# In every step of the attention loop, VectorE makes the low parts of the step behind before the present score's row maximum

## The reference, cut to what matters

```
s_cmp = einsum('bsghd,bcgd->bsghc', qg, kcmp) * scale      # compressed keys
p_cmp = masked_softmax(s_cmp, cmp_mask)
imp = einsum('bsgc,cn->bsgn', p_cmp.sum(axis=3), overlap)  # importance of 64-token blocks
_, sel_idx = lax.top_k(imp, 8)
s_sel = einsum('bqghd,bgqkd->bqghk', q_b, k_sel) * scale   # the 8 chosen blocks
s_w   = einsum('bqghd,bkgd->bqghk', q_b, k_w) * scale      # a window of 512 tokens
o = g[0] * o_cmp + g[1] * o_sel + g[2] * o_w
```

## Time and profile before

| what | value |
|---|---|
| median of three timed runs | 3189.26 us |
| profiled execution, its own time | 3188.89 us |
| its span | 3187.2 us |
| TensorE matmul busy, share of span | 3064.1 us, 96% |
| TensorE weight load busy | 2489.2 us, 78% |
| VectorE busy | 1985.1 us, 62% |
| ScalarE busy | 1339.1 us, 42% |
| GpSimd busy | 1898.0 us, 60% |
| granted TensorE clock, mean | 0.992 |

### The profile page before, as it was taken

One profiled execution on the slowest core, in us unless ns is written; L12 is line 12 of the kernel. 1 busy time (PEld: TensorE's weight loads), 2 busy tenths in 40 slices (PEclk: granted clock), 3 DMA queues, 4 the chain that ended last, 5 costly groups with the idle time before them and its releaser, 6 DMA issues.

```text
span 3187.2 us, 40487 instructions
## 1 busy us (share of the span) xinstructions
PE 3064.1 (96%) x14709; PEld 2489.2 (78%) x14709; DVE 1985.1 (62%) x2563; ACT 1339.1 (42%) x2285; POOL 1898.0 (60%) x1601
## 2 busy tenths in 40 slices
PE   8999999998999999999999999999989999999998
PEld 6888887676787888788778788867668778878887
DVE  7872256887757565655678532678775765466555
ACT  2124414766314555433320342257661345564333
POOL 3557632324456777998745585323333578889985
PEclk8999999999999999999999999999999999999999
DMA  7454551001433666644334447200005335575432
GB/s 254 151 164 128 152 132 27 1 1 34 174 91 113 212 211 211 214 158 149 128 132 139 145 146 187 73 8 1 34 21 180 110 121 184 170 235 205 155 116 106
DMA packets 378861, 412.04 MB, mean 129 GB/s; under 512 B 13355, under 2 KB 302375, under 8 KB 374312
## 3 DMA queue, kind: packets, MB, share of 16 engines
q1 hardware_dynamic: 327922, 274.77, 28.5%
q10 hardware_dynamic: 50742, 134.68, 11.9%
HBM read 294.06 MB, written 108.00 MB: 126 GB/s over the span
## 4 chain that ended last, share of the span: by engine, by line
PE 66%; DVE 13%; POOL 9%; DMA 5%; issue 3%; ACT 3%; SPq 0%; ACTq 0%; POOLq 0%; DVEq 0%
PE lin L1603 26%; PE lin L1722 24%; POOL wsum L1512 4%; POOL unit L1516 4%; PE aux L1896 2%; DVE pTL L2895 2%; DMA xraw<-in_w_ff 2%; PE lin L2038 2%; DMA wraw<-in_w_ff 2%; DVE negm L2871 2%; PE pv L1912 2%; PE pv L1913 1%; PE lin L1872 1%; PE lin L1943 1%; DVE adared L760 1%
## 5 line engine op out<-in xcount | busy, mean ns | idle before, releaser
L1722 PE MATMUL lin<-hH,unit 128*128 128x512 f32 x1712 | 565.7, 394 | 17.2 <-ACT fbuf L2440 6.6
L1443 POOL TENSOR_SCALAR unit<-wraw 128x512 fp32r<-128x512 f32 x228 | 188.0, 825 | 563.2 <-PE lin L1603 262.3
L1722 PEld LDWEIGHTS lin<-hH,unit 128*128 128x128 f32 x1712 | 323.9, 189 | 90.1 <-issue 15.4
L1516 POOL TENSOR_TENSOR unit<-wsum,unit 128x512 fp32r<-128x512 f32 x226 | 326.1, 1443 | 62.6 <-ACT unit L2161 62.0
L1445 POOL TENSOR_TENSOR wlo<-wraw,unit 128x512 fp32r<-128x512 f32 x228 | 337.9, 1482 | 19.0
L1722 PE MATMUL lin<-hL,unit 128*128 128x512 f32 x856 | 335.4, 392 | 0.0
L3079 DVE SCALAR_TENSOR_TENSOR xT<-lin,adac,xT 128x512 f32<-128x512 f32 x256 | 186.7, 746 | 216.0 <-PE lin L1722 192.2
L1603 PE MATMUL lin<-hH,unit 128*128 128x512 f32 x928 | 301.0, 394 | 5.6 <-POOL wlo L1445 5.6
L1603 PE MATMUL lin<-hL,unit 128*128 128x512 f32 x928 | 296.8, 390 | 0.0
L1603 PE MATMUL lin<-hH,wlo 128*128 128x512 f32 x928 | 296.6, 390 | 0.0
L1461 POOL TENSOR_SCALAR prob<-prob,fac 128x640 f32<-128x640 f32 (+3 forms) x128 | 112.8, 881 | 296.8 <-DVE fac L2865 287.8
(11 more groups left out here) (432 smaller groups left out, 7548.6 us busy)
## 6 DMA issues: line engine op xcount, KB each, us to landing
wraw<-in_w_ff SPq DMA_DIRECT2D x110, 512.0 KB, 6.4
wraw<-in_w_in SPq DMA_DIRECT2D x72, 512.0 KB, 5.0
wraw<-in_w_ada SPq DMA_DIRECT2D x56, 512.0 KB, 4.4
hid_keep<-ropes ACTq DMA_DIRECT2D x28, 1024.0 KB, 8.4
hN<-hid_keep SPq DMA_DIRECT2D x24, 1024.0 KB, 7.2
mix_keep<-tmp ACTq DMA_DIRECT2D x32, 512.0 KB, 6.0
hid_keep<-fbuf ACTq DMA_DIRECT2D x14, 1024.0 KB, 4.3
xraw<-in_w_ff SPq DMA_DIRECT2D x26, 512.0 KB, 8.7
```

The lines of the kernel that those rows point to most:

```text
L1443: pool.tensor_scalar(high, raw, 1.0, 1.0, ALU.mult, ALU.mult).then_inc(w_hi, 1)
L1516: pool.tensor_tensor(wide_part(n, i, 1), x, wide_part(n, i, 0).bitcast(F32), ALU.subtract).then_inc(form_lo, 1)
L1722: mm = pe.matmul(bank, w[:, k * P:(k + 1) * P], m[:, k, :], start=WIDE_BEGINS[i] and w is wh and m is mh and k == 0, stop=w is wl and k == ...
```

## The change

In step u VectorE's program now begins with the low parts of the groups of step u-1 (they stand at L2887 in the changed kernel), and the row maximum of unit u (or the three operations of a `c` unit) comes second. Before, it was the other way round. The waits are the same, and so are all instructions; TensorE, ScalarE, GpSimd and the DMA queues have the same rows in the same order as before.

```diff
                 for u in range(len(STEPS)):
+                    for x in STEPS[u - 1] if u else []:
+                        if x["kind"] != "b":
+
+                            r = SEEN[x["qt"]] if x["kind"] == "c" else P
+                            dve.wait_ge(t_hi, past["t_hi"] + x["v_no"] + 1)
+                            dve.tensor_tensor(pt("low", x, r), turned(x, r), pt("high", x, r).bitcast(F32),
+                                              ALU.subtract).then_inc(t_free[x["bank"]], 1)
                     if 0 < u < len(UNITS):
                         if UNITS[u][0] == "c":
                             dve.wait_ge(s_done, past["s_done"] + u + 2)
...
                             maximum(u)
                     if u == 2:
                         v_low("vs", vs, pv[:, :, :].rearrange("p g n -> p (g n)")).then_inc(v_lo, 2)
-                    for x in STEPS[u - 1] if u else []:
-                        if x["kind"] != "b":
-
-                            r = SEEN[x["qt"]] if x["kind"] == "c" else P
-                            dve.wait_ge(t_hi, past["t_hi"] + x["v_no"] + 1)
-                            dve.tensor_tensor(pt("low", x, r), turned(x, r), pt("high", x, r).bitcast(F32),
-                                              ALU.subtract).then_inc(t_free[x["bank"]], 1)
                     for st in SETS:
                         if st["last"] + 1 == u:
                             factors(st)
```

## The result

The changed kernel takes 3316.7 us (median of four runs, 3314.19 to 3323.1) beside 3188.03 us for the kernel before on the same chip. The ratio over all runs is 1.0408 (that of the two medians 1.0404), with a 95% interval of 1.0394 to 1.0422: 4.1% slower, where 3301 us and the range 3260 to 3345 had been forecast. The profiled execution has a span of 3311.9 us, 124.7 more than before.

What follows compares the result with a forecast made beforehand. TensorE sets the pace with VectorE close behind, but the change closes a ring through ScalarE and VectorE. 62 + 8 - 14 = +56 us per layer, +112 for two, on 3188.9 gives 3301 us, range 3260 to 3345.

Steps and rivals of the forecast that it cites:

- The ring: Floor under steps with groups: exponential, high parts, low parts, next maximum, next exponential; 3.49 us at 640 columns, two groups.
- Term 1: The 90 attention steps with groups per layer lengthen from 224.1 us to at least 286.1: +62.0 us per layer.
- the floor of 286.1: Least time in us per layer for the 90 steps with groups: exponentials 64.8, maxima 72.6, the rest 148.8.
- Term 2: Steps where VectorE's other work exceeds ScalarE's part, mainly three with compressed probabilities per layer: +8 us, bounds 6 to 12.
- Term 3: The 44 steps without groups per layer, 23 right behind a step with groups, shrink: -14 us, bounds 0 and -20.
- The clock: Rival: TensorE's share in attention drops and its clock halves in a quarter of the stage; 3400 us, chance 0.05.
- The drain rule: VectorE's next operation waits until the one ahead leaves the pipeline: 0.08 us more per handover, 12 us per layer, 3325 us.
- The rival for faster: TensorE's 16.6 us per layer of attention waits for low parts vanish and decide: 3156 us, chance 0.03.

Runs made afterwards that it cites:

- the singles' kernel: In the changed kernel, low parts go ahead of the maximum only in steps with exactly one, behind it otherwise; 3247.6 us, ratio 1.0181 to the kernel before.

## Why the prediction was right

- **The ring.** As predicted, and to 0.03 us where nothing else intrudes: 3.46 us at 640 columns and two groups (3.49 worked out), 3.94 at 896 (3.96), 2.86 with one group at 640 (2.89). The run of fifteen steps from 21 to 36 took 55.5 us; 54.1 had been added up, and 43.1 had been the time before. The shortened maximum, the shortened low part and the single low part first each change the step by what the ring says, and giving the maximum of the next unit instead opens it. In the first layer 62 of the 90 steps with groups take between 0.08 us less than their ring and 0.02 more. (The run from step 21 to 36 is not the whole run of steps with groups, as the description of the kernel has it: step 20 has one group too. The sum over the fifteen is not touched by that.)
- **Term 1, +62.0.** The 90 steps with groups took 303.7 us in the first layer, 17.6 above the floor of 286.1. The floor itself held; the 17.6 are in the next points, less about 2 for handovers that were 0.03 us shorter than taken.
- **Term 2, +8.** Too large: the six steps behind compressed units ran 4.6 us over their floor, and a smaller one 0.5. After its maximum VectorE began the compressed probabilities at once, and they took 3.3 us to the first low part instead of 3.9. One row makes up most of that, L2823. Its time in the kernel before, then the changed kernel's time line:

```profile
610.16 1.06 DVE L2823 TENSOR_TENSOR tmp<-tmp,cst 128x376 f32<-128x376 f32 x1
```

```profile
631.06 0.53 DVE L2812 TENSOR_REDUCE cst<-tmp 128x8 f32<-128x376 f32 x1
...
631.87 0.55 DVE L2823 TENSOR_TENSOR tmp<-tmp,cst 128x376 f32<-128x376 f32 x1
...
634.03 0.43 DVE L2920 TENSOR_TENSOR atL<-tmp,atH 128x256 fp32r<-128x256 f32 x1
634.37 1.28 DVE L2887 TENSOR_TENSOR pTL<-aux,pTH 128x512 fp32r<-128x512 f32 x2
635.57 1.08 DVE L2871 TENSOR_REDUCE negm<-lin 128x1 f32<-128x896 f32 x1
```

  This step takes 5.45 us beside 5.38 before: here the new order costs 0.07 us. With L2823 as long as before it would be about 0.5 us more, an estimate from these two rows. The prediction had no term for a row that changes its own length.
- **Term 3, -14.** The term that was mis-sized. The 44 steps without groups went from 64.7 to 49.3 us, -15.4, as sized. But "the step after needs a score that waits for the exponential before, so some comes back" was nearly all: the steps with groups that follow a step without ran 10 us over their floor. Step 54 of the changed kernel (ScalarE, TensorE and ScalarE again):

```profile
710.58 0.79 ACT L2351 ACTIVATE prob<-lin,negm 128x640 f32<-128x640 f32 x1 [1.18 <-DVE negm L2871]
...
711.52 0.50 PE L1872 MATMUL lin<-ksH,qS 128*128 128x512 f32 x1 [0.37 <-ACT prob L2351]
...
711.65 0.79 ACT L2351 ACTIVATE prob<-lin,negm 128x640 f32<-128x640 f32 x1 [0.18 <-DVE negm L2871]
...
712.74 0.60 PE L1891 MATMUL aux<-ident,tmp 128*39 128x128 f32 x4
...
713.37 0.59 ACT L2382 ACTIVATE pTH<-aux 39x512 fp32r<-39x512 f32 x1 [0.84 <-PE aux L1891]
```

  Step 53 was quick, 1.07 us. But its exponential frees the bank for the next score, the transposition is queued behind that score, and the high part waits 0.84 us for it. The same wait of the high part stands in 12 of the 23 steps of this kind, 8.5 us in all, and makes up most of the 10. Net, term 3 is about -5.
- **The clock** was a rival with 0.05, and in part it came. In the changed kernel's attention it fell to 1.2 GHz for 3 to 7 us at a time, five times in the first layer (about 24 us in all) and seven in the second. The first of them:

```profile
555.00:560.00 5.00, 3.72 (x24) 3.10 (x23) 3.17 (x5) 1.91 (x5) 0.00 (x0) 0.86 0.00 0
560.00:565.00 5.00, 5.00 (x17) 3.40 (x17) 2.69 (x6) 1.49 (x4) 0.00 (x0) 0.50 0.00 0
```

  Before the fall TensorE had gaps of 0.54, 0.16 and 1.12 us. Steps 11, 12, 62 and 63, which lay in or beside such stretches, ran 4.3 us over their floor. In the second layer 12, 62 and 63, with no fall beside them, ran 0.05 us under it, so there the clock is the cause. The falls near 791 and 862 us were hidden by slack; step 105, counted under term 3, took 0.74 us more than in the second layer. The mean over the stage was 0.97, not a half clock. What sets off a fall is not shown: in 51 of the 134 steps TensorE had a gap of 0.5 us or more, and the longest, 1.80 us before 706.41, stood in a stretch of granted clock 1.00 (700 to 712 us). The Trainium skill, TensorE: Matmul & The Clock Gate, section "HAM oscillation — how this bites in real kernels", describes a wait that comes back before every block of products and throttles the clock each time. The trace agrees only in part: the falls come again, but behind few of the gaps, with a price near 4 us in the first layer where the rival had 50.
- Together, 62 - 2 + 5 + 10 - 15 + 4 = +64 us per layer. The forecast's +56 was low by what came back in term 3 (9 us) and by the clock (4), and high by 3 in term 2 and by 2 in handovers. That these partly cancelled is luck.
- **The drain rule.** The estimate by the rule of the Trainium skill, VectorE: DVE Perf Modes, section "The DRAIN you can't avoid", was 3325 us. The same section says that a next operation that is not held starts earlier. The median of 3316.7 lies between 3325 and 3301, but the row decides: in the ring a maximum starts 1.20 us behind two low parts of 1.29 (619.17 to 620.37), still 0.09 before their end. The sum was short elsewhere.
- **Two signs failed.** TensorE's waits for low parts were to be nearly gone; they are 22.0 us where they were 16.6. A low part that stands first in its step is still late if the whole step is: in ring steps where it waits it waits 0.16 to 0.20 us, behind compressed units 0.88 to 1.17, and in several steps of the narrower tiles up to 1.49. Their total says little about the order. TensorE's waits of scores for exponentials did come, 23.8 us. And TensorE was to be busy for 77% of the stage and was for 82%: its 309.9 us had been put at 284, as before. Some 24 us at half the clock explain 12 of these 26 us at most; the rest is open.
- **The rival for faster** fell with the run behind the compressed probabilities: earlier low parts in the very steps with the longest waits gave a ratio of 1.0003.

## What to carry to other kernels

Before two instructions of an in-order queue change places, follow each through the other engines until it comes back to the same queue; if the one put first waits for something that the one put second leads to, a ring closes and its length is a floor under every step that holds both. Here that ring's length, added up from single rows, gave the step to 0.03 us, while totals of waits pointed the other way. And where one engine sets the pace and does the same work in either order, as VectorE behind the compressed probabilities, a shorter wait of another engine is worth nothing.

## What the runs showed of the hardware that was not expected

TensorE's granted clock, 1.00 throughout the attention of the kernel before, fell to 0.50, 1.2 GHz, twelve times for 3 to 7 us in the two attentions of the changed one. In the first layer the falls stood behind gaps of 0.2 to 1.4 us in a row and not, as near 1005 us of the kernel before, beside one long wait:

```profile
1005.21 0.77 PE L1722 MATMUL lin<-hH,unit 128*128 128x512 f32 x1 [3.28 <-ACT fbuf L2440]
```

In the second layer the falls lay at other steps than in the first, under the same order of work.

One VectorE instruction, L2823 on 128x376 elements, took 1.06 us in the kernel before and 0.55 us in the changed one. In the kernel before GpSimd multiplied probabilities beside it (a run of four, 607.35 to 610.83 us), in the changed one GpSimd's run of four had ended at 631.72 us, just before it began. In the singles' kernel it took 0.55 us with GpSimd busy throughout, but there the instruction behind it, L2826, took 0.95 us where it took 0.55 in the two kernels above. That the two engines hinder each other would fit all three; no run tests it.
